# A two-layer S5/gMLP decoder step on one core: first mixer's norm and products reordered, B table work and one-hots moved

## The reference

```
h = RMSNorm(x);  z = h @ w_in            # columns: u (512), ub (512), v (512)
group A: S5 state space model on u       # complex diagonal recurrence, y = Re(C s) + D u, GELU, GLU
group B: gMLP gating                     # gelu(ub) * (tril(W_s) @ LayerNorm(gelu(v)) + b)
x = x + [RMSNorm(yA), RMSNorm(yB)] @ w_out
x = x + FFN(RMSNorm(x))                  # layer 0 dense SwiGLU, layer 1 top-2 of 8 SwiGLU experts
```

## Time and profile before

| | us |
|---|---|
| median of 3 runs | 863.03 (862.31 to 868.1) |
| profiled execution | 862.85, span 861.0 |
| PE busy | 823.1 (96%) |
| DVE busy | 551.2 (64%) |
| ACT busy | 402.0 (47%) |
| POOL busy | 212.4 (25%) |

### The profile page before, as it was taken

The page is one execution under the profiler, slowest core; times in us unless marked ns, Lnnn a source line. Parts: engine busy times, 40 slices in busy tenths (PEclk is TensorE's granted clock), DMA queues, the critical chain, the costliest instruction groups (busy, mean ns, idle before and its releaser), DMA issues.

```text
span 861.0 us, 13804 instructions
## 1 busy us (share of the span) xinstructions
PE 823.1 (96%) x5086; PEld 641.7 (75%) x5086; DVE 551.2 (64%) x1006; ACT 402.0 (47%) x607; POOL 212.4 (25%) x182
## 2 busy tenths in 40 slices
PE   9998999999989999999999999999999998999985
PEld 7586779999989999848777888887776442865322
DVE  8978567566956556467952799799836131963115
ACT  7786444455324441278241488667634021750111
POOL 3800123221324422525112004314214000141002
PEclk9999999999989999999999899999999999999997
DMA  9600904755546531550310399988989999999992
GB/s 304 193 1 4 351 26 136 225 165 160 164 136 165 166 116 50 170 180 4 138 68 1 146 421 348 368 291 301 375 323 384 423 420 421 421 413 422 421 412 96
DMA packets 89458, 200.77 MB, mean 233 GB/s; under 512 B 26240, under 2 KB 48016, under 8 KB 89392
## 3 DMA queue, kind: packets, MB, share of 16 engines
q1 hardware_dynamic: 88464, 198.86, 63.1%
q10 hardware_dynamic: 576, 0.59, 0.2%
q0 software_dynamic: 352, 0.44, 0.2%
HBM read 198.25 MB, written 1.61 MB: 232 GB/s over the span
## 4 chain that ended last, share of the span: by engine, by line
PE 69%; DVE 14%; DMA 6%; SPq 5%; issue 3%; ACT 2%; POOL 1%; DVEq 0%; ACTq 0%; POOLq 0%
PE ps L1336 7%; PE ps L1335 7%; PE ps L1337 7%; PE ps L1524 5%; SPq L769 5%; DMA wraw_d<-in_moe_w_gate 4%; PE ps L1350 4%; PE ps L1414 4%; PE ps L1636 4%; PE ps L1637 3%; PE ps L1639 3%; PE ps L1652 3%; PE ps L1779 2%; PE ps L1780 2%; PE ps L1783 2%
## 5 line engine op out<-in xcount | busy, mean ns | idle before, releaser
L1335 PE MATMUL ps<-Md,split_u 128*128 128x288 f32 (+2 forms) x304 | 89.7, 295 | 0.0
L1337 PE MATMUL ps<-Md,split_u 128*128 128x288 f32 (+2 forms) x304 | 89.1, 293 | 0.0
L1836 DVE TENSOR_TENSOR xb<-xb,ps 128x288 f32<-128x288 f32 x80 | 33.3, 450 | 64.8 <-PE ps L1524 26.5
L829 POOL TENSOR_TENSOR wrnd_g<-wraw_g,wrnd_g 128x1024 fp32r<-128x1024 f32 (+1 forms) x6 | 20.9, 3491 | 181.1 <-ACT wrnd_g L1008 181.1
L1836 DVE TENSOR_TENSOR wrnd_g<-wraw_g,wrnd_g 128x1376 fp32r<-128x1376 f32 (+2 forms) x31 | 48.3, 1577 | 14.3 <-ACT wrnd_g L1008 14.1
L1336 PE MATMUL ps<-hbr,split_u 128*128 128x288 f32 (+1 forms) x192 | 57.1, 297 | 0.0
L1337 PEld LDWEIGHTS ps<-Md,split_u 128*128 128x128 f32 (+2 forms) x304 | 56.9, 187 | 0.0
L1335 PEld LDWEIGHTS ps<-Md,split_u 128*128 128x128 f32 (+2 forms) x304 | 56.8, 187 | 0.1
L1002 ACT ACTIVATE split_u<-raw 128x1024 fp32r<-128x1024 f32 (+2 forms) x38 | 39.7, 1049 | 36.1 <-PE ps L1337 36.1
L1836 DVE TENSOR_TENSOR wrnd_u<-wraw_u,wrnd_u 128x1376 fp32r<-128x1376 f32 (+2 forms) x34 | 56.3, 1686 | 0.0
L1836 DVE TENSOR_TENSOR wrnd_d<-wraw_d,wrnd_d 128x1376 fp32r<-128x1376 f32 (+2 forms) x20 | 34.0, 1730 | 34.5 <-ACT wrnd_d L1008 34.5
(11 more groups left out here) (469 smaller groups left out, 2184.0 us busy)
## 6 DMA issues: line engine op xcount, KB each, us to landing
wraw_g<-in_moe_w_gate SPq DMA_DIRECT2D x31, 688.0 KB, 10.3
wraw_u<-in_moe_w_up SPq DMA_DIRECT2D x29, 688.0 KB, 17.5
wraw_d<-in_moe_w_gate SPq DMA_DIRECT2D x22, 688.0 KB, 9.4
wraw_g<-in_moe_w_down SPq DMA_DIRECT2D x28, 512.0 KB, 15.6
wraw_u<-in_moe_w_down SPq DMA_DIRECT2D x28, 512.0 KB, 13.1
raw<-in_ffn_w_gate SPq DMA_DIRECT2D x20, 512.0 KB, 4.4
raw<-in_ffn_w_up SPq DMA_DIRECT2D x20, 512.0 KB, 4.1
raw<-in_ffn_w_down SPq DMA_DIRECT2D x20, 512.0 KB, 4.1
```

The costliest lines, as they stand in the source:

```text
L1335: pe.matmul(out, w_hi, x_hi, start=start, stop=False)
L1337: return pe.matmul(out, w_lo, x_hi, start=False, stop=stop)
L1836: return dve.tensor_tensor(o, a, b, op)
```

## The change

Seven edits; the numbers of `sum_ready` that later waits name go up by one and are left out of the diff.

1. The first 512 KB of w_in (k = 0, 1) get a transfer of their own (`w_first`), k = 2, 3 another. Four warm-up matmuls go.
2. The first half of u runs k outside, q inside. In the first layer the squares are summed by eight matmuls with 32 columns of ones, four of them side by side in four groups of 32 output partitions of bank 6; ACT copies the bank, and one full matmul adds the groups after the first bank of u's second half.
3. ACT negates C ahead of r_tok, takes the standard deviation one step later in the first layer, and does the GELUs of ub behind the table copies.
4. DVE in the first layer: `scaled_u` right behind the reciprocal, the fourth C power behind the statistics, and the first half of the scan without `gate_rows` in it; these and the layer norms follow it.
5. POOL's masks of the first layer wait for the first v tile.
6. The eight `b_part` steps move from chunks 32 to 38 and 63 to 69 to chunks 41 to 56.
7. `pair_one_hots` moves from the first step of the final part into the loop's second unit, step 2.

```diff
-B_AT = (32, 34, 36, 38, 63, 65, 67, 69)
+B_AT = (41, 44, 45, 48, 49, 52, 53, 56)
 B_LOAD = 14
...
-WARM_START = 18
+WARM_START = 14
 SCATTER_BANK = (3, 4, 5, 6, 7, 6, 7, 6)
...
                     load_x(0)
-                    piece(0, 0, 4, 0)
+                    sp.dma_start(w_in[:, 0:2, 0:MIX], src[:, 0:2, 0:MIX]).then_inc(w_first, 16)
+                    piece(0, 2, 4, 0)
                     sp.dma_start(b_raw, b_d[l]).then_inc(prep_in, 16)
...
                 pool.wait_ge(mix_in, 80 * (l + 1))
+                if l == 0:
+                    pool.wait_ge(v_ready, 1)
                 up_b = upper.unsqueeze(1).to_broadcast([P, NH, QC])
...
-                for s in range(0 if l else 2):
-                    spread_b(s)
-                root(4 * l, 7, DM, r_mix)
+                if l == 0:
+                    spread_b(0)
+                    act.wait_ge(part_mm, 1)
+                    act.activation(partial, bank(6), ACT.Copy).then_inc(sum_ready, 1)
+                    spread_b(1)
+                root(4 * l, 7, DM if l else NSAMP * DM, r_mix)
                 for s in range(2, 2 if l else CH):
                     spread_b(s)
-                act.wait_ge(rt_mm, l + 1)
-                for t, (_, n) in enumerate(TILES):
-                    act.activation(r_tok[0:n, t:t + 1], ps[0:n, 7, T + t:T + t + 1], ACT.Copy).then_inc(rt_ready, 1)
                 if l:
...
                 act.activation(CPX[:, 1, :, 0, :], CPX[:, 1, :, 0, :], ACT.Copy, scale=-1.0).then_inc(cn_ready, 1)
+                act.wait_ge(rt_mm, l + 1)
+                for t, (_, n) in enumerate(TILES):
+                    act.activation(r_tok[0:n, t:t + 1], ps[0:n, 7, T + t:T + t + 1], ACT.Copy).then_inc(rt_ready, 1)
...
                 for q in range(MT):
-                    if q == (2 if l else 0):
+                    if q == (2 if l else 1):
                         act.wait_ge(var_ready, l + 1)
...
                     ce.then_inc(cp_ready, 1)
-                for q in range(MT):
-                    act.wait_ge(ubr_ready, 4 * l + q + 1)
-                    act.activation(ub[:, q, :], ub[:, q, :], ACT.Gelu_apprx_tanh).then_inc(ub_ready, 1)
                 act.wait_ge(const_in, 32)
...
                                    ACT.Copy).then_inc(kc_ready, 1)
+                for q in range(MT):
+                    act.wait_ge(ubr_ready, 4 * l + q + 1)
+                    act.activation(ub[:, q, :], ub[:, q, :], ACT.Gelu_apprx_tanh).then_inc(ub_ready, 1)
                 for q in range(MT):
...
         def _(pe):
-            def mean_sum(src, k0, n, b, need):
-
-                for k in range(n):
-                    pe.wait_ge(sq_ready, need + k + 1)
-                    mm = pe.matmul(bank(b), ones, src[:, k0 + k, :], start=(k == 0), stop=(k == n - 1))
-                mm.then_inc(ms_mm, 1)
-
             def mean_pair(src, k, b, need, sums):
...
             for l in range(DEPTH):
-                def u_half(k0):
-
+                def u_product(q, k):
+
+                    return pe.matmul(bank(q), w_in[:, k, q * P:(q + 1) * P], h[:, k, :],
+                                     start=(k == 0), stop=(k == KT - 1), skip_group_check=True)
+
+                for k in range(4):
+                    pe.wait_ge(h_ready, 24 * l + k + 1)
+                    if k == 0 and l == 0:
+                        pe.wait_ge(w_first, 16)
+                    if k == (0 if l else 2):
+                        pe.wait_ge(w_in_in[0], 16 * (l + 1))
                     for q in range(MT):
-                        for k in range(k0, k0 + 4):
-                            if q == 0:
-                                pe.wait_ge(h_ready, 24 * l + k + 1)
-                                pe.wait_ge(w_in_in[k // 4], 16 * (l + 1))
-                            mm = pe.matmul(bank(q), w_in[:, k, q * P:(q + 1) * P], h[:, k, :],
-                                           start=(k == 0), stop=(k == KT - 1), skip_group_check=True)
-                        if k0:
-                            mm.then_inc(ua_mm, 1)
-
-                u_half(0)
+                        if l and k == 0 and q:
+                            pe.wait_ge(h_ready, 24 + q + 1)
+                        u_product(q, k)
                 if l == 0:
-                    mean_sum(sq0[0], 0, KT, 7, 0)
-                if l:
+                    for k in range(KT):
+                        g = k % 4 * NSAMP
+                        pe.wait_ge(sq_ready, k + 1)
+                        mm = pe.matmul(ps[g:g + NSAMP, 6, 0:T], ones[:, 0:NSAMP], sq0[0][:, k, :],
+                                       start=(k < 4), stop=(k >= 4), skip_group_check=True)
+                    mm.then_inc(part_mm, 1)
+                else:
                     pe.wait_ge(xadd, X_DENSE[1] + 8)
-                    mean_pair(sq0[1], KT - 1, 7, 32, 4)
-                u_half(4)
+                    mean_pair(sq0[1], KT - 1, 7, 32, 5)
+                for q in range(MT):
+                    for k in range(4, KT):
+                        if q == 0:
+                            pe.wait_ge(h_ready, 24 * l + k + 1)
+                            pe.wait_ge(w_in_in[1], 16 * (l + 1))
+                        mm = u_product(q, k)
+                    mm.then_inc(ua_mm, 1)
+                    if l == 0 and q == 0:
+                        pe.wait_ge(sum_ready, 1)
+                        pe.matmul(bank(7), ones, partial, start=True, stop=True).then_inc(ms_mm, 1)
                 pe.wait_ge(r_ready, l + 1)
...
                         pe.wait_ge(vp_ready, l + 1)
-                        pe.wait_ge(sel_ready, 1)
                         pe.matmul(ps[0:NSAMP, 4, :], sel, vpart, start=True, stop=True,
...
                         if q == 2:
-                            pe.wait_ge(oh_ready, i + 2)
+                            pe.wait_ge(oh_ready, i * 2 + 1)
                             pe.wait_ge(xadd, each(i, a, 8, X_MOE))
...
                             if k == 4:
-                                pe.wait_ge(oh_ready, i + 2)
+                                pe.wait_ge(oh_ready, i * 2 + 2)
                             elif k == 5:
...
                 if l == 0:
+                    dve.wait_ge(const_in, 32)
+                    dve.tensor_reduce(sel, ident.rearrange("p (g i) -> p i g", i=NSAMP), AX.X, ALU.add)
                     root_inverse()
-                    dve.wait_ge(const_in, 32)
-                    dve.tensor_reduce(sel, ident.rearrange("p (g i) -> p i g", i=NSAMP), AX.X, ALU.add).then_inc(sel_ready, 1)
+                    scaled_u()
                     rotation_powers(sv)
                     magnitudes()
-                    scaled_u()
                 link(dve.memset(stat, 1.0))
...
                 if l == 0:
-                    for s in range(CH):
+                    for s in range(CH - 1):
                         tight_c_power(s)
-                    dve.wait_ge(c_powers, 1)
                     dve.wait_ge(mix_in, 80)
...
                         last.then_inc(var_ready, 1)
+                if l == 0:
+                    tight_c_power(CH - 1)
                 dve.wait_ge(std_ready, l + 1)
...
                     link(tt(wi, wi, tmp, ALU.subtract))
-                    if q == 0:
+                    if (l, q) == (0, 1):
+                        gate_rows(3)
+                    if (l, q) == (1, 0):
                         gate_rows(0)
...
                     link(dve.tensor_tensor_scan(wi, mg, wi, 0.0, ALU.mult, ALU.add))
-                    if q == 0:
-                        for t in range(3 if l else 0):
+                    if (l, q) == (1, 0):
+                        for t in range(3):
                             layer_norm(t)
...
                     link(tt(or_, or_, v8(tmp), ALU.subtract))
-                    if q == 0:
+                    if (l, q) == (1, 0):
                         gate_rows(2)
...
                     if q == 0:
-                        for t in range(0 if l else 3):
-                            layer_norm(t)
-                        gate_rows(3)
+                        if l == 0:
+                            gate_rows(0)
+                            gate_rows(1)
+                            for t in range(3):
+                                layer_norm(t)
+                            gate_rows(2)
+                        else:
+                            gate_rows(3)
                 dve.wait_ge(st_ready, 2 * (l + 1))
...
                 for q in range(len(steps)):
-                    if a == 0 and q == (0 if final else 3):
+                    if not final and a == 0 and q == 3:
                         dve.wait_ge(gather_mm, i * 4 + 4)
-                        if final:
-                            pair_one_hots()
-                        else:
-                            one_hots(i * 2 + 2)
+                        one_hots(i * 2 + 2)
+                    if not final and a == 1 and q == 2:
+                        dve.wait_ge(gather_mm, i * 4 + 8)
```

(12 more changed lines are left out.)

4 lines of the change are left out of this document (2 added, 2 removed).

## The result

The changed kernel took 855.38 us (median of 5 runs, 854.92 to 857.46) against 863.03, a ratio of 0.9915 with a 95% interval of 0.989 to 0.9939. Run again beside other kernels it had 856.03 and a ratio of 0.9938 (0.9916 to 0.996). It is faster by 6 to 8 us, where 15 were forecast; the range of 843.5 to 856 held the time near its upper end, but the gain is only half of the forecast one, since one step that was priced at nothing cost 9.5 us.

The account below looks back on a forecast made before the run. PE was taken as the bound, busy for 823.1 of 861.0 us. First mixer -8.4, dense FFN -5.4 and experts -0.8 sum to -14.6 from 862.85, forecast 848 us, range 843.5 to 856.

Parts of the forecast that it names:

- First mixer, start: First mixer's u: earlier w_in transfer and column-group square sums let PE end u at 24.45 instead of 27.92, 3.5 us earlier.
- First mixer, DVE and layer norm: First mixer: statistics end at 50.0, ub starts 4.1 us earlier, layer norm's wait and slow stretch give -4.3; mixer sum -8.4.
- Dense FFN, middle: Dense FFN's middle: with no B steps ahead of the addition, 2.31 us idle and 3.1 of slow stretch go, -5.4.
- Dense FFN, second half: Dense FFN's second half: the eight B steps fit DVE's idle time and the low parts' lead, hidden, cost 0.
- The rival on the other side: Dense FFN's second half: DVE falls behind beside POOL, 12.6 us idle plus 13.6 of slow stretches, 874 us; chance 0.05.
- Experts: One-hots' move: -3.6 us at the final part's start, 2.0 back as PE wait in the loop; -0.8 taken.

Follow-up runs that it names:

- 10: The kernel before with only the eight B steps moved to chunks 62 to 69: 858.73 us, ratio 0.9976.
- 11: The kernel before with only the pair one-hots moved behind the output rows of the loop's second unit: 858.88 us, ratio 0.9964.
- 13: The kernel before with only the B steps moved to the change's chunks (41 to 56): 871.77 us, ratio 1.0095.
- 14: The kernel before with only the pair one-hots moved to the loop's second unit, step 2, as changed: 860.84 us, ratio 0.9969.
- experiment 3: The changed kernel with all eight B steps at chunks 62 to 69, behind the last hidden rows: 846.43 us, ratio 0.983.
- experiment 1: The changed kernel with B steps and pair one-hots back at their old places, so the first mixer's edits alone: 851.49 us, ratio 0.9876.
- 12: The changed kernel with one B step of each second-half pair moved to where DVE waits for ACT within the hidden rows: 850.13 us, ratio 0.9842.

## Why the prediction was wrong

- **First mixer, start: right.** 3.5 forecast, 3.93 measured: the transfer landed at 6.4 instead of 6.8, and the sums took 1.11 instead of 1.25, with both switches between full and column-group matmuls in that time. The Trainium skill (TensorEngine Tiling (Array Packing), section Key Properties) says that changing the tiling mode drains TensorE; no cost of that can be seen here, so the time went by the row and not by the rule.
- **First mixer, DVE and layer norm: right.** C powers 28.5 forecast, 28.34 measured; statistics 50.0 and 49.9; ub 53.2 and 52.8; layer norm 68.6 and 67.9; in sum -8.4 and -9.05. What the profile of before did not show is that its wait of 1.11 us has a slow stretch behind it in the other four profiles with that order (10, 11, 13, 14), which the change also removes: in the ten profiles with the whole changed mixer the granted clock is full from 20 to 230 us; the sum was made from one run in which it had none. Taken alone the start would have been worth less than nothing, so the terms were no sum of independent gains.
- **Dense FFN, middle: right.** -5.4 forecast for idle time and slow stretch; measured -11.31 + 9.05 = -2.26 for the idle time, and 2.8 for the slow stretch, by the second half's length of 107.75 before against 104.98 in experiment 3, which has no wait in it: -5.1. In experiment 1 the same stretch cost only 1.5 (106.48).
- **Dense FFN, second half: this step failed.** "There DVE was busy for 30.04 of 53 us", "+ 8 x 2.25 = 48.0", "with half of eight that is 56.8, 3.8 over 53, and the low parts are written seven chunks of 3.2 us ahead (`NSPLIT`), a lead of over 20 us: hidden." It took 23 us of DVE's idle time as room. Part of these are waits for ACT inside the hidden rows, at which queued steps cannot run: 7.42 us in four passes stayed idle. And the lead of the low parts covers only low parts: the scaling of the hidden rows has none, since it can't start before PE ends a pass, and PE needs its banks back one pass later. It stands in DVE's queue behind the B steps, and PE's wait of 7.08 us is for that scaling (`rs_sg`), not for a low part, for which the prediction told the reader to look. The collisions were priced about right, 4 x 2.2 = 8.8 for eight steps against 7.15 for seven; what was missing is that with no lead they and the steps' own time come through to PE: 45.65 + 7.15 + 7.42 = 60.22 us, where PE needs 51. The forecast 0 was +9.5 us (105.0 against 114.4). The rival on the other side had this very mechanism, DVE behind in the second half, with a price of 26 and a chance of 0.05; POOL's contention that it rested on is in the trace with 5.50 us for 1.09. That agrees with the Trainium skill (GPSIMD Engine Reference, Specifications), by which GpSimd shares its SBUF interfaces with VectorE.
- **Experts: right.** -3.7 behind the one-hots' old place, +1.96 at the new one, -1.7 in sum, the end without a slow stretch in the loop; forecast -0.8 between -1.6 and +0.1. The wait of 1.09 + 0.60 came in two pieces and had no slow stretch behind it.

The sum with the measured terms is -9.05 - 5.1 + 9.45 - 1.7 = -6.4, against -6.5 in the profile and -7.65 in the medians; what the account has besides (2.1 lost up to the first unit's hidden product, 0.3 of it won back behind it, 1.9 won behind the third unit's, 1.6 of them at the end) nearly cancels. That the sum comes out says little for the single terms of the first mixer and of the middle, since the clock behind the same waits differs from profile to profile. With that one term at +9.5 instead of 0 the forecast would have been 857.7.

## What to carry to other kernels

An in-order engine's idle time is room only where the work put in can run: sort its idle time by what ended it, and count as room, per pass, only the wait ahead of the step that another engine waits for. A lead of buffers protects only what is written ahead; find the step on that queue that has none. The same work put into gaps of the chain itself (12) cost 4.5 us instead of 9.5. And a wait that is shortened or moved may change its granted clock, so a gain upstream of an engine that does not follow can end as a loss.

## What the hardware showed that was not expected

- The same wait of 1.1 us ahead of the same matmuls had a stretch at a granted clock of half behind it in the profiles of 10, 11, 13 and 14 (L1406 in 6.87 us in 11) and none in that of before (3.76 us). Waits of 1.09 and 0.60 us in the changed kernel's experts had none.
- DVE's operations beside POOL's: 5.50 us for 1.09, and 2.98 for 0.85. Either engine can be the one that is held up: POOL's low part took 2.41 us when it came into DVE's comparisons, which then took 2.98, and 6.10 when it came just behind them, with DVE's low parts beside it at their usual length (two in 3.09).
- Eight matmuls of 288 columns in four column groups took 1.11 us, where eight full ones took 3.88: 3.5 times as fast.
